# Router on unnormalised activations, and high-by-high products first, in a two-layer hybrid decoder step

## What is computed

```python
def rmsnorm(x, g):
    y = xf * lax.rsqrt(jnp.mean(xf * xf, axis=-1, keepdims=True) + EPS)
    return (y * g.astype(jnp.float32)).astype(x.dtype)

def moe_swiglu(h, router_w, wg, wu, wd):       # h = rmsnorm(x, ln_ffn_o)
    logits = (h @ router_w).astype(jnp.float32)
    top_v, top_i = lax.top_k(logits, TOP_K)
    gates = jax.nn.softmax(top_v, axis=-1)
    comb = jnp.sum(jax.nn.one_hot(top_i, N_EXPERTS, dtype=jnp.float32) * gates[..., None], axis=-2)
    for e in range(N_EXPERTS):
        out = out + comb[..., e:e + 1].astype(h.dtype) * swiglu(h, wg[e], wu[e], wd[e])
```

## Time and profile before

| | |
|---|---|
| median of 3 runs | 2016.13 us (2015.2 to 2018.71) |
| profiled execution, its own time | 2019.81 us |
| its span | 2018.2 us |
| mean granted clock | 0.909 |
| busy: PE, PEld, DVE, ACT, POOL | 90%, 77%, 68%, 51%, 2% |
| moved by DMA | 445.51 MB, 221 GB/s on average |
| first expert begins (L2007) | 965.2 us from the span's start |

### The profile page before, as it was taken

The page is one execution under the profiler, slowest core; times in us unless marked ns, Lnnn a source line. Parts: engine busy times, 40 slices in busy tenths (PEclk is TensorE's granted clock), DMA queues, the critical chain, the costliest instruction groups (busy, mean ns, idle before and its releaser), DMA issues.

```text
span 2018.2 us, 25558 instructions
## 1 busy us (share of the span) xinstructions
PE 1809.0 (90%) x9872; PEld 1544.3 (77%) x9872; DVE 1363.1 (68%) x1577; ACT 1038.1 (51%) x956; POOL 41.0 (2%) x92
## 2 busy tenths in 40 slices
PE   4966879998997776977999999999999999999998
PEld 3945779998995765657887887887878878788786
DVE  3564234354775654653788887888878888888786
ACT  3442133343553221012676776776767677667574
POOL 2011000000001000000000000000000000000000
PEclk9975789997997888566999999999999999999999
DMA  6343134443342001312698997998989989899894
GB/s 198 134 167 99 42 124 169 134 179 131 126 167 70 1 1 49 98 52 85 251 375 312 322 375 273 370 334 316 370 285 358 365 293 367 324 329 366 288 363 169
DMA packets 199084, 445.51 MB, mean 221 GB/s; under 512 B 9457, under 2 KB 20883, under 8 KB 198959
## 3 DMA queue, kind: packets, MB, share of 16 engines
q1 hardware_dynamic: 182206, 423.75, 58.5%
q0 software_dynamic: 3872, 12.85, 2.3%
q10 hardware_dynamic: 12924, 7.77, 1.3%
HBM read 437.28 MB, written 7.29 MB: 220 GB/s over the span
## 4 chain that ended last, share of the span: by engine, by line
PE 78%; DVE 11%; ACT 4%; PEld 2%; issue 2%; DMA 1%; ACTq 1%; PEldq 0%; DVEq 0%
PE bank L2022 15%; PE bank L2007 10%; PE bank L2008 10%; PE bank L2009 10%; PE bank L760 5%; PE bank L761 5%; PE bank L762 5%; PE bank L1981 2%; DVE weight_lo L468 2%; PE bank L705 1%; ACT weight_hi L465 1%; PE bank L1859 1%; PE bank L1991 1%; PE bank L1854 1%; DVE work L1317 1%
## 5 line engine op out<-in xcount | busy, mean ns | idle before, releaser
L468 DVE TENSOR_TENSOR weight_lo<-weight_ring,weight_hi 128x2048 fp32r<-128x2048 f32 (+1 forms) x358 | 810.2, 2273 | 346.6 <-ACT weight_hi L465 346.6
L465 ACT ACTIVATE weight_hi<-weight_ring 128x2048 fp32r<-128x2048 f32 (+1 forms) x358 | 680.2, 1904 | 382.7 <-PE bank L762 151.9
L2007 PE MATMUL bank<-weight_hi,h_lo 128*128 128x512 f32 x896 | 359.8, 402 | 23.4 <-DVE work L1579 19.7
L2008 PE MATMUL bank<-weight_lo,h_hi 128*128 128x512 f32 x896 | 354.2, 395 | 0.0
L2009 PE MATMUL bank<-weight_hi,h_hi 128*128 128x512 f32 x896 | 353.8, 395 | 0.0
L760 PE MATMUL bank<-h_hi,weight_lo 128*128 128x264 f32 x1072 | 313.6, 293 | 26.0 <-DVE h_lo L740 14.2
L761 PE MATMUL bank<-h_lo,weight_hi 128*128 128x264 f32 x1072 | 310.9, 290 | 0.0
L762 PE MATMUL bank<-h_hi,weight_hi 128*128 128x264 f32 x1072 | 308.9, 288 | 0.0
L760 PEld LDWEIGHTS bank<-h_hi,weight_lo 128*128 128x128 f32 x1072 | 208.1, 194 | 32.4 <-DVE h_lo L740 15.8
L2007 PEld LDWEIGHTS bank<-weight_hi,h_lo 128*128 128x128 f32 x896 | 171.3, 191 | 60.3 <-issue 23.6
L761 PEld LDWEIGHTS bank<-h_lo,weight_hi 128*128 128x128 f32 x1072 | 208.0, 194 | 0.0
(11 more groups left out here) (420 smaller groups left out, 1753.7 us busy)
## 6 DMA issues: line engine op xcount, KB each, us to landing
weight_ring<-in_moe_wg SPq DMA_DIRECT2D x104, 1024.0 KB, 6.5
weight_ring<-in_moe_wu SPq DMA_DIRECT2D x96, 1024.0 KB, 6.9
weight_ring<-in_moe_wd SPq DMA_DIRECT2D x88, 1024.0 KB, 6.3
work<-in_moe_wd SPq DMA_DIRECT2D x24, 1024.0 KB, 6.9
weight_ring<-in_w_in_o SPq DMA_DIRECT2D x8, 2048.0 KB, 8.6
work<-in_moe_wu SPq DMA_DIRECT2D x16, 1024.0 KB, 6.1
weight_ring<-in_w_in_e SPq DMA_DIRECT2D x5, 2048.0 KB, 13.7
weight_ring<-in_ffn_wg SPq DMA_DIRECT2D x5, 2048.0 KB, 7.7
```

Source lines behind the costliest of these rows:

```text
L465: return SC.activation(whi[:, p % SPLIT, 0:size], src, ACT.Copy).then_inc(sig("hi_done"), 1)
L468: V.tensor_tensor(wlo[:, p % SPLIT, 0:size], src, whi[:, p % SPLIT, 0:size].bitcast(F32), ALU.subtract)\
L2007: PE.matmul(out, hte_l[:, j, :], hi[:, jj, :], start=j == 0, stop=False)
L2008: PE.matmul(out, hte_h[:, j, :], lo[:, jj, :], start=False, stop=False)
```

## The change

Two things are changed. **(1) High first.** In all split products PE waits for the high part of a piece, does the products that need no low weights, and only then waits for the low part; dense products also start on the activations' high half. `combine` uses banks 7, 5 and 6, waits for both halves of the output, and the wait for `added` moves from step 1's g product to step 0's down product. **(2) Router.** The logits are made from `xT` times the gain, not normalised, as nine rows: eight of logits and one that sums squares (through a selector `pick`, from squares that POOL added up tile by tile). Half of the row blocks are multiplied between the two pieces of the last `w_out_o` chunk. ACT copies the nine rows, PE transposes them, DVE takes the top two of the unnormalised logits, and ACT scales `h_tok` as it copies it. Transposes of `hT` come beside the top two; those of `xT` come half before and half after the first dispatch; the gates and combine weights come after the first selection. On ACT the copies to `acc`, the high part of a piece and the exponential stand before the first `dispatch_out`.

```diff
@@ dense_chunk
-                pe.wait_ge(*at("lo_done", p + 1))
+                pe.wait_ge(*at("hi_done", p + 1))
...
+                        PE.matmul(out, hi[:, jj, cols_], h_hi[:, j0 + j, :], start=first and j == 0, stop=False)
+                    if c == 0:
+                        pe.wait_ge(*at("lo_done", p + 1))
+                    for jj in range(half):
+                        PE.matmul(out, lo[:, jj, cols_], h_hi[:, j0 + part * half + jj, :], start=False, stop=False)
+                    if c == 0 and low and part == 0:
+                        pe.wait_ge(*at(*low))
+                    for jj in range(half):
+                        j = part * half + jj
+                        last = PE.matmul(out, hi[:, jj, cols_], h_lo[:, j0 + j, :], start=False, stop=last_one and j == k - 1)
...
+                if part == 0 and between:
+                    between()
@@ gpsimd
+            for m in range(1, KD):
+                gp.wait_ge(*at("norm3_sq", m + 1))
+                if m > 1:
+                    gp.wait_ge(*at("norm3_sum", m - 1))
+                GP.tensor_tensor(inv[:, 0, :], inv[:, 0, :], inv[:, m, :], ALU.add).then_inc(sig("norm3_sum"), 1)
@@ scalar
-            norm_act_squares(act_e, 3, ("out_o_added", KD))
-            norm_act_root(act_e, 3)
...
+            router_squares(range(HALF, KD))
+            act_e.wait_ge(*at("lg_psum", 1))
+            SC.activation(lg_row, bank[3][0:NE + 1, 0:T], ACT.Copy).then_inc(sig("lg_row"), 1)
+            act_e.wait_ge(*at("logits", 1))
+            SC.activation(rstd[:, 0:TT], logit[:, 0:TT, NE], ACT.Sqrt, bias=eps_t[:], scale=1.0 / D)
...
+            for k in range(YC):
+                for i, (t0, n) in enumerate(TOK):
+                    act_e.wait_ge(*at("htok_psum", k * NTT + i + 1))
+                    SC.activation(h_tok[0:n, i, k * CHUNK_COLS:(k + 1) * CHUNK_COLS], bank[k * 4 + i][0:n, :], ACT.Copy,
+                                  scale=rstd[0:n, i:i + 1]).then_inc(sig("htok"), 1)
+            behind(dense_hi, act_e, "w_out_o", 1, 1)
...
@@ vector
+                dve.wait_ge(*at("out_o_added", m + 1))
+                V.tensor_scalar(hT[:, m, :], xT[:, m, :], col("ln_ffn_o", m), None, ALU.mult).then_inc(sig("router_h"), 1)
...
-            norm_dve(dve, 3, "ln_ffn_o", link)
...
+            V.reciprocal(rstd, rstd).then_inc(sig("norm3_inv"), 1)
+            experts = iota[:, 0:NE].unsqueeze(1).broadcast_to([P, NTT, NE])
+            for k in range(2):
+                last = V.tensor_tensor(idx_pair[:, k], experts, idx_f[:, :, k:k + 1].broadcast_to([P, NTT, NE]), ALU.is_equal)
+            link(last)
+            V.tensor_tensor(mask, idx_pair[:, 0], idx_pair[:, 1], ALU.add).then_inc(sig("masks"), 1)
@@ tensor
-            pe.wait_ge(*at("norm2_done", 2))
+            pe.wait_ge(*at("norm2_hi", 2))
...
-            pe.wait_ge(*at("on_lo", 2))
-            dense_pe(pe, "w_out_o", KD, "out_o_psum", "out_o_added")
-
-            norm_pe(pe, 3)
...
+            dense_pe(pe, "w_out_o", KD, "out_o_psum", "out_o_added", low=("on_lo", 2),
+                     between=lambda: router_logits(range(HALF)))
+            router_logits(range(HALF, KD))
+            pe.wait_ge(*at("norm3_sum", KD - 1))
+            PE.matmul(bank[3][0:NE + 1, 0:T], pick[:, 2 * HC - 1 - NE:2 * HC], inv[:, 0, :], start=False, stop=True)\
+              .then_inc(sig("lg_psum"), 1)
...
+                        PE.matmul(out, hte_h[:, j, :], hi[:, jj, :], start=False, stop=False)
+                    wait_low(it, kind, c, part)
...
             def down(it, c):
...
                     pe.wait_ge(*at("y_out", (it + 1) * YC))
+                    pe.wait_ge(*at("added", (it + 1) * (NTT * YC)))
...
-                pe.wait_ge(*at("y_out", (it + 1) * YC + hf + 1))
+                pe.wait_ge(*at("y_out", (it + 2) * YC))
...
-                    out = bank[(7, 3, 2)[i]]
+                    out = bank[(7, 5, 6)[i]]
...
-                    if c == 1:
-                        pe.wait_ge(*at("added", (it + 1) * (NTT * YC)))
...
                 dispatch(0, r)
+            token_rows(xT, 1, "xtok_psum")
             pe_expert(0, False, True)
```

More of the change, by code:

```diff
@@ L740, in low_parts, with dense_chunk @@
                 V.tensor_tensor(h_lo[:, part, :], src[:, part, :], h_hi[:, part, :].bitcast(F32), ALU.subtract).then_inc(sig(done), 1)
-        def dense_chunk(pe, name, n, tiles, bank_of, out_sig, before, j0=0, first=True, last_one=True):
+        def dense_chunk(pe, name, n, tiles, bank_of, out_sig, before, j0=0, first=True, last_one=True, low=None, between=None):
             i = place[name, n]
@@ L767, in dense_chunk, with dense_pe @@
                 last.then_inc(sig("piece_used"), 1)
-        def dense_pe(pe, name, tiles, out_sig, free_sig, before=()):
+                if part == 0 and between:
+                    between()
+        def dense_pe(pe, name, tiles, out_sig, free_sig, before=(), low=None, between=None):
             def wait_bank(m):
@@ L778, in dense_pe @@
             for n in range(-(-tiles // per)):
-                dense_chunk(pe, name, n, range(n * per, min(tiles, (n + 1) * per)), lambda m: m % 8, out_sig, wait_bank)
+                dense_chunk(pe, name, n, range(n * per, min(tiles, (n + 1) * per)), lambda m: m % 8, out_sig, wait_bank,
+                            low=low if n == 0 else None, between=between if n else None)
         @block.scalar
@@ L1512, in _ @@
-            last.then_inc(sig("masks"), 1)
-            dve.wait_ge(*at("ranks_psum", 1))
-            V.reduce_max(count, bank[6][:, NTT * NE:(NTT + 1) * NE], X)
-            for i, (t0, n) in enumerate(TOK):
-                last = V.scalar_tensor_tensor(rank[0:n, i, :], mask[0:n, i, :], -FAR, bank[6][0:n, i * NE:(i + 1) * NE], ALU.mult, ALU.add)
+            link(V.tensor_copy(idx_f, top_i[:, :, 0:2]))
+            dve.wait_ge(*at("norm3_root", 1))
+            V.reciprocal(rstd, rstd).then_inc(sig("norm3_inv"), 1)
@@ L1946, in _ @@
+            dense_pe(pe, "w_out_o", KD, "out_o_psum", "out_o_added", low=("on_lo", 2),
[4 more added lines that the diff above has]
+              .then_inc(sig("lg_psum"), 1)
+            pe.wait_ge(*at("lg_row", 1))
             for i, (t0, n) in enumerate(TOK):
-                for j in range(KD):
-                    last = PE.matmul(bank[5][0:n, i * NE:(i + 1) * NE], hT[:, j, t0:t0 + n], w_router[:, j, :],
-                                     start=j == 0, stop=j == KD - 1)
+                last = PE.transpose(bank[3][0:n, T + i * (NE + 1):T + (i + 1) * (NE + 1)], lg_row[:, t0:t0 + n], ident[0:NE + 1, 0:NE + 1])
@@ L1962, in _ @@
+            for k in range(YC):
+                token_rows(hT, k, "htok_psum")
             pe.wait_ge(*at("masks", 1))
@@ L2007, in product @@
                         PE.matmul(out, hte_l[:, j, :], hi[:, jj, :], start=j == 0, stop=False)
[L2008 to L2009 removed]
+                        PE.matmul(out, hte_h[:, j, :], hi[:, jj, :], start=False, stop=False)
+                    wait_low(it, kind, c, part)
+                    for jj in range(KD // 2):
+                        j = part * (KD // 2) + jj
+                        last = PE.matmul(out, hte_h[:, j, :], lo[:, jj, :], start=False, stop=j == KD - 1)
                     last.then_inc(sig("piece_used"), 1)
```

184 lines of the change are left out of this document (98 added, 86 removed).

## The result

The changed kernel takes 1952.18 us (median of 4, 1950.87 to 1953.45) against 2017.42 us (2015.2 to 2020.52) of the kernel before on the same chip: ratio 0.9676, interval 0.9659 to 0.9692, 65.2 us less. The forecast was 1953.0. The profiled execution took 1950.87 us with a span of 1949.2 us and a granted clock of 0.921 (before 0.909).

A forecast was written before the change was run, and what follows sets the result against it. PE was taken as the bound (78% of the chain). Savings of 35.6 - 0.6 + 7.2 + 21.0 = 63.2 us from 2019.8 gave 1956.6, shifted 3.7 to the median: 1953, range 1944 to 1959, with rivals 1943 to 1967.

The forecast's parts named there:

- Experts, 35.6 less 0.6: Seven boundaries between experts: moving the wait for `added` saves 35.6 us; the final `combine`'s wait for both halves loses 0.6.
- The walk: Piece-by-piece timing of low weight parts at an expert boundary: nothing late, the tightest piece 2.4 us early.
- Dense, 7.2 and 1.3 for `w_out_o`: Dense products starting on the high half: 7.2 us saved without `w_out_o`, whose earlier start saves 1.28 us, counted under router.
- Router, 21.0: From `w_out_o`'s wait to the first expert: 21.0 us saved, `w_out_o`'s earlier start included.
- the hT transposes: Router, PE: 24 transposes taken at the lower clock, 5.38 us, ending at 926.4; at the higher clock 923.9.
- the hole of 4.16 us: Behind the first dispatch: ACT's copies, table load, exponentials and `dispatch_out`, with DVE's low half, take 4.2 us; PE idles over 4.
- The cold router: Rival: router at clock 0.50 throughout, slower dispatch and `xT` transposes, 5.8 us, 1959; chance 0.12.
- The wait between experts: Rival: low parts late at six expert boundaries, half of the gain (18 us) gone, 1971; chance 0.05.
- The router's chain: Rival: engine handoffs and POOL make the router's chain 6 to 9 us longer than walked, 1961; chance 0.13.
- DMA: Rival: DMA becomes the bound in the experts, needing a limit under 350 GB/s; chance 0.02.
- The pace with another stationary operand each time: Rival, slower: without repeated operands a matmul takes 16 ns more; 65 us on experts, 2069 with dense products; chance 0.03.
- The waits that were moved: Rival: the change does not do what it says, every new wait standing where the old one did; chance 0.01.

The follow-up runs named there:

- The ladder: Four kernels on one chip: before 2018.0, only the new router 1999.3, with the experts' edits 1964.3, with the dense edits too 1955.0 us.
- The first experiment: Changed kernel with the wait for `added` back before step 1's gate product and `combine` on banks 7, 3, 2; 1993.51 us, ratio 0.988.
- the router alone: Changed kernel with both old product orders and the old wait for `added`, only the new router left; 1999.25 us, ratio 0.9916.
- the first four experiments: Changed kernel with old `added` wait (1993.51 us), old experts' product order (1955.01), old dense order and waits (1964.28), or all three undone (1999.25).
- the last experiment: Changed kernel with the experts' old product order and one more DVE instruction ahead of a low part at each expert boundary; 1966.89 us, ratio 0.9743.

## Why the prediction was right, point by point

**Experts, 35.6 less 0.6: right.** The ladder gives 35.0, the traces 32.6 for six boundaries and 3.5 for the last and the end, 36.1. The 1.1 us between forecast and traces is one term: for what stays of a boundary I took 5.48 us, and it is 5.32, seven times. The walk said nothing would be late; PE is busy for 49.85 of 50 us at a boundary, and the seventh piece's low part is 2.2 us early, where the walk had 2.5. The 0.6 us for the late second half of the output is there: L2094 waits 2.1 us, and 1.5 with the old wait put back. The first experiment's 38.5 holds 5 us that its trace spends ahead of the first expert; behind it the edit is worth 35.6 us in that pair of traces.

**Dense, 7.2 and 1.3 for `w_out_o`: right.** 9.3 by the ladder, 9.1 by the waits, and `w_out_o` starts 8.1 us sooner (890.8 to 882.7). `w_in_o`'s waits for low weights shrank by 1.5 us (3.4 to 1.9), not by 1.0.

**Router, 21.0: two terms mis-sized, 5 us short in the traces.** I walked 52.2 us from the end of the second high half to the first expert; it took 48.3 (882.6 to 930.9). The term that failed is the hT transposes, taken at the lower clock because PE idles three times just before: they took 2.84 us, not 5.38, at clock 1.00. The one idle piece that the trace shows there, 0.47 us, did not lower it. The rest, 1.4 us, is 0.3 in `w_out_o`, 0.5 from there to these transposes, and 0.6 from them to the dispatch. POOL's addition took 0.74 us where I took 0.6 between 0.4 and 0.9; the estimate of 0.58 from the Trainium skill's figure ("GPSIMD Engine Reference", 3.1) was short by the same, which would fit a fixed part in each instruction. Against the gain stands the hole of 4.16 us, forecast at 4.2, and the half clock after it, forecast at 2.6 and measured at 1.47. The gain is thus 27.5 us from the high half to the first expert, less 1.5: 26 in this pair of traces, where I had 21.0. Both hold the 1.3 us of `w_out_o`'s earlier start, which the ladder counts with the dense products; without them it is 24.7 in this pair, 23.8 in the trace of the router alone, and 18.8 by the ladder's medians, against a forecast of 19.7. The two traces of the last comparison differ by 23.3 us in all and the medians by 18.8: the router's profiled execution is the fastest of its four (2.7 us under their median), and the one of the kernel before lies 1.8 above the median of this chip. Which of the two is nearer to the router's worth was not settled.

**The spread between the two.** Up to `w_out_o` the changed kernel and six of the experiments run the same code there, and reach it at 882.7, 886.9, 883.0, 885.7, 884.3, 883.8 and 883.2 us; the kernel before and the two with the old dense order reach it at 890.8, 894.0 and 889.8. Single profiled executions differ by 4 us there without any edit. Of the 4.3 us of the first experiment, 3.3 arise in the last 17 us: two groups of matmuls of the `on_root` sums run at the half clock there and take 6.58 and 7.18 us instead of 5.45 and 4.99. Of the 3.1 us of the kernel with `dispatch_out` first, 2.7 are there at 256 us, in part as longer waits for the first loads. The second group in the changed kernel and in the first experiment:

```profile
873.53 4.99 PE L1979 MATMUL bank<-work,ident 8*128 8x264 f32 x16 [2.39 <-DVE work L1501]
```
```profile
875.60 7.18 PE L1979 MATMUL bank<-work,ident 8*128 8x264 f32 x16 [2.39 <-DVE work L1501]
```

At the end it is the same. PE waits 1.83 us ahead of the last down product in all ten traces. In five of them the clock stays at 1.00 behind it; in the five of the first four experiments and of the kernel with `dispatch_out` first it falls, and from that wait to the last `combine` it takes 1.6 us longer (9.4 against 7.8). Four matmuls each behind it, in the changed kernel and in the one with `dispatch_out` first:

```profile
1931.33 1.21 PE L2079 MATMUL bank<-weight_hi,h_lo 128*128 128x512 f32 x4 [1.83 <-DVE h_lo L1571]
```
```profile
1930.23 1.91 PE L2082 MATMUL bank<-weight_hi,h_lo 128*128 128x512 f32 x4 [1.83 <-DVE h_lo L1574]
```

What decides whether it falls was not found out.

**Sum.** My 63.2 us was against 2019.8 and then shifted by 3.7 to the median. The profiled executions differ by 68.9 us (2019.81 to 1950.87), so the sum was 5.7 short of that pair: 5.0 in the router and 1.1 in the experts, less 0.4 in the dense products; and the changed kernel's profiled execution lies 1.3 below its median, where the one before lay 3.7 above. The forecast met the median within 1 us because these two offset each other, which is luck; the fair figures are 63.2 expected and 65.2 between the medians, 63.0 by the ladder.

**Rivals.** The cold router (1) did not come: clock 1.00 from 912 to 926. The wait between experts did not come back (2). The router's chain was shorter, not longer (3). DMA at 348 to 368 GB/s in the windows ended no wait at a boundary (4). The pace with another stationary operand each time is that of before, 228 matmuls in 50 us (5); in the old `down` four matmuls of six repeat it, not every second one as I wrote, which leaves the argument as it is. The waits that were moved are gone from their old places (6).

## What to carry to other kernels

Look for the wait that stands before work which doesn't need it and move it to the first instruction that does: that was over half of the gain, for one moved wait and other banks for the scattered output. Reordering products so that late operands come last gains nothing where they aren't late, but it gives slack, which can be measured by giving the producer more work, or read from the traces as the time between the end of the producer's instruction and the start of the first one that needs it. When a chain is shortened, look at what was pushed behind its end: here three copies and a table load that used to be hidden stood in front of the instruction that was waited for; they cost 5.5 us, and only had to stand behind it.

## What the runs showed of the hardware

**Idle time and clock.** What a short idle stretch costs is not fixed by its length. The seven stretches of up to 1.67 us at the boundaries of the last experiment left the clock at 1.00. The one of 1.83 us at the end left it there in five traces of ten and lowered it in the other five, at a cost of 1.6 us beyond itself. Six boundaries of the kernel before, 3.3 us idle, cost 1.7 to 3.1 us beyond it (10.28 to 11.69 us, less 3.28 and the 5.32 that stay in the changed kernel), and one of 4.16 us cost 1.47.

**POOL beside DVE.** The first of POOL's additions took 2.23 us, its likes 0.74. It lay beside a low part on DVE:

```profile
898.94 2.23 POOL L663 TENSOR_TENSOR work<-work 128x264 f32<-128x264 f32 x1 [56.15 <-ACT work L1050]
```
```profile
898.26 2.29 DVE L470 TENSOR_TENSOR weight_lo<-weight_ring,weight_hi 128x2048 fp32r<-128x2048 f32 x1 [0.64 <-ACT weight_hi L467]
```

DVE's instruction ended at 900.55 and POOL's at 901.17, 0.62 us later, about its own duration: it looks as if it could not begin before. It is also POOL's first addition after 56 us of idle time, and in all nine traces with the new router it stands at the same place, so a cost of the first instruction is not ruled out. The Trainium skill ("GPSIMD Engine Reference", 1. Specifications) says that POOL shares its way to SBUF with DVE and contends with DVE instructions of two SBUF inputs, which this one is. It cost nothing here, since the last addition has no low part beside it; with one it would, as an estimate from 2.23 and 0.74, have cost the router up to 1.5 us.
